# A hybrid decoder trunk on one core: state-space products, kernel taps and modulation columns issued in column pieces of TensorE

## The reference, cut to what matters

```python
mod = jax.nn.silu(c) @ ada_w + ada_b                       # 1024 -> 3072, one row
shift, scale, gate = jnp.split(mod[:, None, :], 3, axis=-1)
...
bu = einsum('bsgc,gpc->bsgp', ug, bbar)                    # 32 groups of 16 channels, 64 complex states
x  = associative_scan(x_t = abar * x_(t-1) + bu_t)         # diagonal recurrence along the sequence
y  = einsum('gcp,bsgp->bsgc', c_re, x_re) - einsum('gcp,bsgp->bsgc', c_im, x_im)
```

## Time and profile before

| | |
|---|---|
| median of 3 runs | 1238.48 us (1238.11 to 1239.49) |
| the profiled execution's own time | 1234.73 us |
| its span, first to last instruction | 1232.9 us |
| TensorE matmul busy | 1206.5 us, 98% |
| VectorE busy | 887.1 us, 72% |
| ScalarE busy | 507.2 us, 41% |
| GpSimd busy | 484.5 us, 39% |

### The profile page before, as it was taken

One profiled execution on the slowest core, in us unless ns is written; L12 is line 12 of the kernel. 1 busy time (PEld: TensorE's weight loads), 2 busy tenths in 40 slices (PEclk: granted clock), 3 DMA queues, 4 the chain that ended last, 5 costly groups with the idle time before them and its releaser, 6 DMA issues.

```text
span 1232.9 us, 17087 instructions
## 1 busy us (share of the span) xinstructions
PE 1206.5 (98%) x6532; PEld 965.2 (78%) x6532; DVE 887.1 (72%) x1439; ACT 507.2 (41%) x840; POOL 484.5 (39%) x336
## 2 busy tenths in 40 slices
PE   7999999999999999999999999999999999999998
PEld 4787777787788788888868777778777788888887
DVE  5796789867387776977947588888746877687252
ACT  5355324753443343342343632276353344333331
POOL 0143432243463234545415334423425442255551
PEclk9999999999999999999999999999999999999999
DMA  9442222132322435464615212212323323465322
GB/s 356 172 170 69 53 68 70 52 120 69 103 66 74 136 89 187 158 253 152 232 44 171 86 56 66 69 54 68 123 65 111 87 64 84 138 221 204 90 83 69
DMA packets 63441, 141.84 MB, mean 115 GB/s; under 512 B 29440, under 2 KB 31744, under 8 KB 62592
## 3 DMA queue, kind: packets, MB, share of 16 engines
q1 hardware_dynamic: 54016, 137.61, 34.5%
q10 hardware_dynamic: 9344, 3.15, 1.0%
HBM read 127.89 MB, written 10.49 MB: 112 GB/s over the span
## 4 chain that ended last, share of the span: by engine, by line
PE 91%; DVE 5%; ACT 1%; issue 1%; DMA 1%; POOL 0%; SPq 0%; DVEq 0%; ACTq 0%
PE bank L1679 24%; PE bank L1681 24%; PE bank L1680 24%; PE bank L1866 2%; PE bank L1821 2%; PE bank L1831 1%; PE bank L1845 1%; PE bank L1690 1%; PE bank L1920 1%; PE bank L1935 1%; PE bank L1953 1%; PE bank L1954 1%; DVE arena L1483 1%; PE bank L1838 1%; PE bank L1927 1%
## 5 line engine op out<-in xcount | busy, mean ns | idle before, releaser
L727 POOL TENSOR_TENSOR w_lo<-raw,w_hi 128x512 fp32r<-128x512 f32 (+1 forms) x166 | 240.2, 1447 | 727.9 <-ACT w_hi L761 727.7
L1679 PE MATMUL bank<-h_hi,w_hi 128*128 128x512 f32 x896 | 361.9, 404 | 4.7 <-ACT arena L838 2.6
L1681 PE MATMUL bank<-h_hi,w_lo 128*128 128x512 f32 x896 | 349.3, 390 | 0.0
L1680 PE MATMUL bank<-h_lo,w_hi 128*128 128x512 f32 x896 | 349.0, 390 | 0.0
L761 ACT ACTIVATE w_hi<-raw 128x1024 fp32r<-128x1024 f32 (+2 forms) x170 | 178.7, 1054 | 223.8 <-PE bank L1681 180.5
L728 POOL TENSOR_TENSOR w_lo<-raw,w_hi 128x512 fp32r<-128x512 f32 (+2 forms) x166 | 251.6, 1516 | 0.0
L1679 PEld LDWEIGHTS bank<-h_hi,w_hi 128*128 128x128 f32 x896 | 168.3, 188 | 48.7 <-issue 13.0
L1680 PEld LDWEIGHTS bank<-h_lo,w_hi 128*128 128x128 f32 x896 | 168.4, 188 | 38.3 <-issue 4.8
L1681 PEld LDWEIGHTS bank<-h_hi,w_lo 128*128 128x128 f32 x896 | 168.2, 188 | 35.7
L1679 PE MATMUL bank<-w_hi,h_hi 128*128 128x512 f32 (+1 forms) x256 | 97.2, 380 | 3.3 <-issue 1.5
L1680 PE MATMUL bank<-w_lo,h_hi 128*128 128x512 f32 (+1 forms) x256 | 94.9, 371 | 0.0
(11 more groups left out here) (286 smaller groups left out, 1794.6 us busy)
## 6 DMA issues: line engine op xcount, KB each, us to landing
raw<-in_wfull SPq DMA_DIRECT2D x170, 512.0 KB, 3.7
arena<-in_wada SPq DMA_DIRECT2D x48, 512.0 KB, 4.2
x_scratch<-xm SPq DMA_DIRECT2D x2, 2048.0 KB, 8.3
arena<-x_scratch SPq DMA_DIRECT2D x2, 2048.0 KB, 9.8
arena<-in_x SPq DMA_DIRECT2D x4, 512.0 KB, 6.3
arena<-in_s5m SPq DMA_DIRECT2D x2, 1024.0 KB, 6.1
u_scratch<-arena ACTq DMA_DIRECT2D x4, 512.0 KB, 4.4
arena<-u_scratch SPq DMA_DIRECT2D x8, 256.0 KB, 3.8
```

The costliest lines, as they stand in the source:

```text
L727: nc.gpsimd.tensor_tensor(lo[:, :half], raw_chunk(n)[:, :half], hi[:, :half].bitcast(F32), ALU.subtract)
L1679: mm(out_, a_hi, b_hi, start=first, stop=False)
L1680: mm(out_, a_hi, b_lo, start=False, stop=False)
L1681: return mm(out_, a_lo, b_hi, start=False, stop=last)
```

## The change

Four groups of TensorE products are issued in pieces that take only some of the columns of the array and write only some of the output partitions, and one group of copies follows suit. What is computed stays the same.

- Parts 2 and 4: each product with a 128x128 stationary matrix becomes two, with its columns 0 to 63 to output partitions 0 to 63 and its columns 64 to 127 to partitions 64 to 127. The moving operand is the same for both.
- Part 1: the 8 products write to four strips of 32 partitions in turn, in one bank in place of two. The stationary matrix is 32 columns wide (the second 16 belong to the next group, and their rows are not read). ACT copies the strips in four instructions of 16 x 2 x 128.
- Steps `ad1` and `adm`: each product with one column of ones becomes two of 64 columns.
- One bank less is taken from the ring for part 1.

```diff
-    "s5": lambda s: ((), (0, 1, 2, 3), (4,), (6,), (7,), (5,))[s[3]],
+    "s5": lambda s: ((), (0, 2, 3), (4,), (6,), (7,), (5,))[s[3]],
...
+HALVES = (slice(0, 64), slice(64, 128))
+KT_ROWS = 32
...
# ACT, part 1
-                        for q in range(2):
-                            src = wait_full(act, (key, q))
...
-                            nc.scalar.activation(kt[0:GC, 4 * q:4 * q + 4],
-                                                 src[0:GC].rearrange("p (a b) -> p a b", a=4),
-                                                 ACT.Copy).then_inc(read((key, q)), 1)
+                        src = wait_full(act, (key, 0))
...
+                        for at in range(4):
+                            ins = nc.scalar.activation(
+                                kt[0:GC, at:QG:4],
+                                src[KT_ROWS * at:KT_ROWS * at + GC, 0:2 * P].rearrange("p (q b) -> p q b", q=2), ACT.Copy)
+                        ins.then_inc(read((key, 0)), 1)
# TensorE, adm (ad1 likewise)
-                        last = mm(bank[BANKS.uses[key][0]][:, c - 1 + ct:c + ct], ada[:, i // 2 % 2, ct * P:(ct + 1) * P],
-                                  ones[:, 0:1], start=True, stop=True)
+                        for low in (0, COL_HALF):
+                            at = ct * P + low
+                            last = mm(bank[BANKS.uses[key][0]][low:low + COL_HALF, c - 1 + ct:c + ct],
+                                      ada[:, i // 2 % 2, at:at + COL_HALF], ones[:, 0:1], start=True, stop=True)
# TensorE, part 1
-                        for q in range(2):
-                            dst = wait_free(pe, (key, q))
-                            for g in range(4):
-                                last = mm(dst[0:GC, g * P:(g + 1) * P], par[:, 0, QG * j + 4 * q + g],
-                                          ca[:, 4 * q + g, 0:CH].rearrange("p m c -> p (m c)"), start=True, stop=True)
-                            last.then_inc(full((key, q)), 1)
+                        dst = wait_free(pe, (key, 0))
+                        for g in range(QG):
+                            at, q = KT_ROWS * (g % 4), g // 4
+                            first = GC * (QG * j + g)
+                            last = mm(dst[at:at + KT_ROWS, q * P:(q + 1) * P], par_flat[:, first:first + KT_ROWS],
+                                      ca[:, g, 0:CH].rearrange("p m c -> p (m c)"), start=True, stop=True)
+                        last.then_inc(full((key, 0)), 1)
# TensorE, part 2
-                            last = mm(dst[:, g * NCH:(g + 1) * NCH], wt[:, g], u_j[:, g], start=True, stop=True)
+                            for ps in HALVES:
+                                last = mm(dst[ps, g * NCH:(g + 1) * NCH], wt[:, g, ps], u_j[:, g], start=True, stop=True)
# TensorE, part 4
-                            mm(dst[:, a_:a_ + NCH], mt[:, g], u_j[:, g], start=True, stop=False)
-                            last = mm(dst[:, a_ + 1:a_ + NCH], ca[:, g, 1:NPOW].rearrange("p m c -> p (m c)"),
-                                      zz[:, g, 0:NCH - 1], start=False, stop=True)
+                            by_out = ca[:, g, 1:NPOW].rearrange("p m c -> p (m c)")
+                            for ps in HALVES:
+                                mm(dst[ps, a_:a_ + NCH], mt[:, g, ps], u_j[:, g], start=True, stop=False)
+                            for ps in HALVES:
+                                last = mm(dst[ps, a_ + 1:a_ + NCH], by_out[:, ps],
+                                          zz[:, g, 0:NCH - 1], start=False, stop=True)
```

More of the change, by code:

```diff
@@ L1729, in _ @@
                         for kh in range(2):
[L1730 to L1731 removed]
+                            for low in (0, COL_HALF):
+                                at = ct * P + low
+                                last = mm(dst[low:low + COL_HALF, ct:ct + 1], ad_in[4 * b + 2 + kh][:, 0, at:at + COL_HALF],
+                                          ones[:, 0:1], start=kh == 0, stop=kh == 1)
                     last.then_inc(full((step, 0)), 1)
```

11 lines of the change are left out of this document (6 added, 5 removed).

## The result

| | before | after |
|---|---|---|
| median of six runs each | 1237.61 us | 1229.85 us |
| lowest to highest | 1233.74 to 1239.49 | 1226.77 to 1230.15 |
| profiled execution | 1234.73 | 1230.15 |
| its span | 1232.9 | 1228.3 |

After takes 0.9945 of the time of before (95% interval 0.9932 to 0.9957): faster by 5.3 to 8.4 us. Forecast were 1214.4 us and a range of 1210 to 1221. The direction came out, but the time lies 8.9 us outside the range. The two profiled executions lie closer together than the medians, 4.6 us, since that of before is among its fastest and that of after its slowest. One of the further executions of before, beside the experiments, took 6930 us, five times as long as all others, and is left out.

A forecast was written before the change was run, and what follows sets the result against it. TensorE, busy 98% of the span, was taken as the bound. Terms -17.6 - 10.0 + 1.4 - 0.4 + 2.5 = -24.1 us took the profiled 1234.73 to 1210.6; 3.75 more for the median gave 1214.4, range 1210 to 1221 us.

The forecast's parts named there:

- The prices of the pieces: TensorE's costs per half record, switch and strip: parts 2 and 4 save 17.6 us, part 1 saves 10.0.
- rival A: Part 1: only two strips run side by side, saving 6.6 us in place of 10.0; 1216.4 us, chance 0.2.
- the recurrence's price: Parts 2 and 4: 0.029 us per half record, taken from the recurrence's same-shaped halves, against 0.110 per full-width record.
- rival D: Parts 2, 4 and modulation: pieces sharing a moving operand don't overlap, part 1 gains nothing; 1249 us, chance 0.04.
- Modulation: Steps adm and ad1: an adm step takes 0.47 us for 0.36, together 1.4 lost; ad1 gains 0.4.
- New waits: TensorE waits where the other side is not set by what became shorter: 2.5 us in all.
- ACT, quarter 1: Ahead of quarter 1's part 2: TensorE waits 0.65 us for ACT's wt2 copies.
- ACT, quarter 3: Ahead of quarter 3's part 2: TensorE waits 0.25 us for ACT's wt2 copies.
- DVE, quarter 1: At quarter 1's swap product that needs L1225: a wait of 0.2 us at most, put at 0.1.
- Weights, layer 1: After layer 1's last part 4: TensorE waits 0.5 us for a weight chunk loaded behind SP's save.
- The chip's clock is full in the stretch that matters: State-space stretch: clock column reads 1.00, so TensorE work removed comes off the time one for one; no clock loss forecast.
- Rival B: State-space stretch: more waits for DVE cost 2 to 3 us a layer; about 1220 us, chance 0.14.

The follow-up runs named there:

- e13: e2 with four full-width 512-column products, their result overwritten, ahead of quarter 2's part 2: 0.9883 of before, 1220.88 us.
- e16: e3 with SP's save of quarter 1's result ahead of its load of quarter 3's u_j: 0.9863 of before, 1218.65 us.
- e8: The changed kernel with four full-width 512-column products, their result overwritten, ahead of quarter 2's part 2: 0.9935 of before, 1228.17 us.
- e1: The changed kernel with the load of quarter 2's u_j moved ahead of quarter 1's part 2 in the list: 0.9944 of before, 1229.03 us.
- e2: The changed kernel with the load back of quarter 2's result moved between the halves of quarter 3's spreads: 0.9878 of before, 1220.91 us.
- e7: e2 with ACT's copies to wt2 ahead of those to kt: 0.9921 of before, 1226.46 us.
- e4: The kernel before with the load moves of both e1 and e2: 0.9992 of before, 1234.40 us.
- e3: The changed kernel with the load moves of both e1 and e2: 0.9898 of before, 1223.34 us.
- e12: The kernel before with e3's moves, quarter 1's save ahead of quarter 3's u load, and two DVE table steps moved: 1.0138 of before.
- halves only: The kernel before with parts 2 and 4 in halves, part 1 in one strip and modulation full-width: 0.9944 of before, 1229.13 us.

## Why the prediction was wrong

**The prices of the pieces held.** Part 1 was forecast at 0.60 and takes 0.58. Its 16 records start in fours, the four within 0.02 us and one four 0.11 behind the other, so four strips do run side by side, and rival A is dead. (The window of the earlier trace rows, on which the prediction leaned, shows its two records only as begun by 114.40; their starts in the trace are 114.02 and 114.03, so that reading was right.) The half records of parts 4 and 2 move on every 0.029 us, the recurrence's price, with one moving operand for both halves: rival D is dead. The Trainium skill says that matmuls start and end in the program's order (TensorE: Matmul & The Clock Gate, The mechanism). It does not speak of the two passes of a float32 product; read over passes, as the prediction read it, the rule would have left part 1 at 1.03, and the trace doesn't agree with that reading. Parts 4 and 2 take 3.17 without their wait where 3.02 was forecast. Modulation loses 0.06 a step where I had 0.11.

**The step that failed is "New waits": 2.5 us, and only of ACT, DVE and weights.** Its parts against the runs:
- ACT, quarter 1: 0.65 forecast, 1.23 measured. The four copies of half the columns take 1.52, not the 1.1 that I had estimated from their columns. Narrow copies cost 0.38 each where the wide cost 0.475.
- ACT, quarter 3: 0.25 forecast, 0.36 measured.
- DVE, quarter 1: 0.1 forecast for the second swap product. The trace of after has no wait at its line, L1955.
- Weights, layer 1: 0.5 forecast. There is none in after, nor in e13 and e16; in e8 there is one of 0.8. No run takes it alone.
- SP was left out. I asked of every wait what TensorE does before it and what ACT and DVE do, but not what SP's queue does. The load of `u_j` costs 3.8 and 2.8 us, the load back, through DVE's list, 2.2 and 2.6. That is 11.4 us for a term that I had at nothing. e1, e2 and e7 show by moving them that these transfers end the waits, e4 that they were no bound before. What each is worth differs: e2 gets back 8 us, clock included, and e1 alone nothing, since DVE is late too.
- The clock: nothing forecast. "The chip's clock is full in the stretch that matters" was a row of before, and I carried it over. In its profiled execution TensorE had no standstill there but 0.85 us ahead of two first swap products in each layer. Three times at half clock cost 7.1 us by the rows, 6.6 of them within the stretches.

The new waits of 14.2 us and those 6.6 make 20.8 of the 21.0 us that are missing in the stretches. That is as close as such a sum can come: the six pairs of parts 4 and 2 cost 0.15 more each than forecast, which would carry it to 21.7. Between and behind the stretches after is 1.9 us longer than before. The modulation's 0.8 and 0.6 of half clock behind layer 0's stretch are in it; the rest I did not trace to single rows.

**Rival B had the right sign and too small a size.** It put more waits at 2 to 3 us a layer and blamed DVE's list. In the changed kernel the waits begin with transfers; DVE becomes the bound when these are moved (e1, e3). What B reckoned with was there to be read: DVE, busy for 85 of 108 us, has under 10 us of idle time left in a stretch 13 us shorter.

**What stays open.** How much of the half clock's 7 us would come off after's time. e4 and e12 lose nearly half of the length of each such time, with TensorE the bound. e8 and e13 hold the clock and gain nothing that the runs can tell; part of what they win goes to the filler itself and to the next wait. And what the limit behind e16 is: its waits for ACT and DVE are spread over four places, and no run takes them one at a time.

## What to carry to other kernels

Before a step of the bounding engine is shortened, list every wait behind it with its spare, and for each follow what releases it back to something that the shortening moves too; a DMA queue with its own order of issues is a list like any engine's, and it keeps its own pace. A start that comes a tenth of a microsecond later than the pattern of its neighbours, as at 423.98, can mark a spare of zero. And a standstill can cost twice: once as a wait, and again at half clock in the work behind it. In e12 a mere reordering of DVE's steps and SP's transfers lost 17 us that way. Where a wait is taken away, look for the next one behind it before its length is counted as a gain: e1 took away 6.6 us of waiting and came out even.

## What the runs showed of the hardware

- Four strips of 32 columns take float32 products of 128 moving columns four records at a time: 16 records start in four groups 0.11 us apart, the last 0.37 us behind the first, and take 0.58 us up to the transposes. In one strip each record starts 0.109 us behind the one ahead, 1.85 us for 16. The stationary matrices are 32 columns wide in the strips, 16 before.
- An ACT copy of 16x256 takes 0.38 us from start to start, one of 16x512 0.475: half the columns cost four fifths.
- The clock of TensorE fell from 2.4 to 1.2 GHz in or behind waits of 1.8 to 5.5 us, in e12 behind three of 0.5 to 1.7 with products between them, and in e4 behind one of 0.85 that brought no fall in before. It did not fall behind each: halves only kept it through 2.8 us at 461.9, e3 through 3.0 at 1031.9. It stayed at half for 3.4, 6.8, 10.2 or 13.7 us. With TensorE the bound, 3.4 us of it cost 1.65 (e4), 10.2 cost 4.9 and 13.7 cost 6.5 (e12). Four products of 512 columns, put in the wait, kept it up.
- A save of 256 KB landed 2.0 us after its issue when it was issued ahead of a load of 256 KB (e16), and 3.2 us after it when it stood 0.38 us behind that load (e3).
